# Seven chunks of a three-block fp32 network turned by DMA transposes in place of TensorE's, and two parameter loads moved behind a transpose

## What is computed

```python
qa, ka, va, qs, ks, vs = jnp.split(h @ even_w_in, idx, axis=-1)     # layer one's input chunks
...
xb = h @ odd_w_in[:, D:]                                            # layer two
xc = conv_b + sum(conv_w[j] * shift(xb, 3 - j) for j in range(4))   # causal, four taps
r = sigmoid(xc @ gate_w[0] + gate_b[0]); i = sigmoid(xc @ gate_w[1] + gate_b[1])
y = gelu(h @ odd_w_in[:, :D]) * lru_scan(r, i * xc)
```

## Time and profile before

| | |
|---|---|
| median of 3 runs | 3118.76 us (3118.72 to 3119.77) |
| the profiled execution, its own time | 3119.9 us |
| its span | 3118.1 us, 37400 instructions |
| TensorE | 3102.8 us, 14684 matmuls |
| VectorE | 1984.4 us |
| ScalarE | 1557.6 us |
| GpSimd | 265.8 us |
| DMA | 621.55 MB, 199 GB/s |
| TensorE's clock granted | full in every slice (2.4 GHz) |

### The profile page before, as it was taken

How to read it: one execution, slowest core, us unless ns; L and a number is a source line. 1 busy time by engine, 2 the same in 40 slices (tenths; PEclk the granted TensorE clock), 3 DMA queues, 4 the chain that set the end, 5 groups by cost and what they waited for, 6 DMA issues and landing times.

```text
span 3118.1 us, 37400 instructions
## 1 busy us (share of the span) xinstructions
PE 3102.8 (100%) x14684; PEld 2574.0 (83%) x14684; DVE 1984.4 (64%) x2278; ACT 1557.6 (50%) x2157; POOL 265.8 (9%) x330
## 2 busy tenths in 40 slices
PE   9999999999999999999999999999999999999999
PEld 8788888888888888878888888888888888888887
DVE  6677765656565768676574655568986555555455
ACT  6666543444444669554443434563455443444344
POOL 0000000000000020010830006720000000000000
PEclk9999999999999999999999999999999999999999
DMA  7455676766667555667676766777655766666664
GB/s 244 143 158 168 190 221 189 218 201 206 207 201 227 166 186 187 213 184 214 200 214 187 219 201 222 245 230 222 203 155 170 211 204 205 197 201 208 188 211 155
DMA packets 408623, 621.55 MB, mean 199 GB/s; under 512 B 112848, under 2 KB 124544, under 8 KB 408448
## 3 DMA queue, kind: packets, MB, share of 16 engines
q1 hardware_dynamic: 403056, 612.52, 64.3%
q10 hardware_dynamic: 5392, 6.64, 0.7%
HBM read 587.09 MB, written 11.01 MB: 192 GB/s over the span
## 4 chain that ended last, share of the span: by engine, by line
PE 95%; DVE 3%; ACT 1%; issue 1%; DMA 0%; SPq 0%; ACTq 0%; DVEq 0%
PE pair L2303 30%; PE pair L2305 30%; PE pair L2304 30%; DVE lo L1412 1%; PE turn_ps L2334 1%; PE pair L2733 0%; DMA turned_bytes<-tmp 0%; ACT hi L697 0%; PE misc_ps L2639 0%; DVE xt_hl L1761 0%; PE misc_ps L2653 0%; PE pair L2271 0%; PE pair L2622 0%; PE pair L2624 0%; PE pair L2623 0%
## 5 line engine op out<-in xcount | busy, mean ns | idle before, releaser
L1412 DVE TENSOR_TENSOR lo<-raw,hi 128x1024 fp32r<-128x1024 f32 x1084 | 1337.6, 1247 | 713.8 <-ACT hi L697 701.7
L697 ACT ACTIVATE hi<-raw 128x1024 fp32r<-128x1024 f32 x1084 | 1128.9, 1057 | 871.5 <-PE pair L2305 860.3
L2303 PE MATMUL pair<-hi,xt_hl 128*128 128x512 f32 (+1 forms) x2780 | 1089.8, 392 | 5.3 <-DVE lo L1412 3.5
L2305 PE MATMUL pair<-lo,xt_hl 128*128 128x512 f32 (+1 forms) x2780 | 1079.6, 388 | 0.0
L2304 PE MATMUL pair<-hi,xt_hl 128*128 128x512 f32 (+1 forms) x2780 | 1078.8, 388 | 0.0
L2303 PEld LDWEIGHTS pair<-hi,xt_hl 128*128 128x128 f32 x2780 | 522.1, 188 | 117.8 <-DVE lo L1412 5.1
L2305 PEld LDWEIGHTS pair<-lo,xt_hl 128*128 128x128 f32 x2780 | 521.9, 188 | 108.7
L2304 PEld LDWEIGHTS pair<-hi,xt_hl 128*128 128x128 f32 x2780 | 522.4, 188 | 103.6
L2303 PE MATMUL pair<-hi,ht_h 128*128 128x512 f32 x1504 | 586.7, 390 | 0.1
L2305 PE MATMUL pair<-lo,ht_h 128*128 128x512 f32 x1504 | 585.2, 389 | 0.0
L2304 PE MATMUL pair<-hi,ht_l 128*128 128x512 f32 x1504 | 585.2, 389 | 0.0
(11 more groups left out here) (343 smaller groups left out, 1717.6 us busy)
## 6 DMA issues: line engine op xcount, KB each, us to landing
raw<-in_mlp_w SPq DMA_DIRECT2D x512, 512.0 KB, 4.5
raw<-in_w_gate SPq DMA_DIRECT2D x88, 512.0 KB, 4.4
raw<-in_w_up SPq DMA_DIRECT2D x88, 512.0 KB, 4.2
raw<-in_w_down SPq DMA_DIRECT2D x88, 512.0 KB, 4.4
raw<-in_even_w_in SPq DMA_DIRECT2D x68, 512.0 KB, 4.2
raw<-in_odd_w_in SPq DMA_DIRECT2D x64, 512.0 KB, 4.2
raw<-in_w_in SPq DMA_DIRECT2D x64, 512.0 KB, 4.5
raw<-in_even_w_out SPq DMA_DIRECT2D x32, 512.0 KB, 4.2
```

What stands on the lines that cost most here:

```text
L697: nc.scalar.activation(hi[:, r], raw[:, slot], ACT.Copy).then_inc(sems["hi_ready"], 1)
L1412: nc.vector.tensor_tensor(lo[:, r], raw[:, slot], hi[:, r].bitcast(F32), ALU.subtract).then_inc(sems["lo_ready"], 1)
L2303: nc.tensor.matmul(to, xh[:, t0 + k, tok], h[:, k], start=s, stop=False)
L2305: mm = nc.tensor.matmul(to, xh[:, t0 + k, tok], l[:, k], start=False, stop=e)
```

## The change

Seven chunks go the second way: in layer one the chunks with c = 7, 0, 2 and 1, in layer two the convolution's chunks 1, 2 and 3. They carry n = -1, which tells them from the MLPs' chunks. Their transpose lands in `stg` itself (`turned_stg`), which is free once it is parted. From there `bytes_join` writes layer one's chunks straight to `qk0`, and the convolution's to `joined`, which lies in `tmp`. The convolution's first tap (`bytes_conv`, ScalarE) and the others then read `joined`, after j = 3, 4 and 5 in place of 2, 3 and 4, and `ht_h` and `ht_l` follow at j = 6.

ScalarE's evacuation waited for the last split in every chunk once there had been a join; now it does so only in a chunk with a parted chunk before it (`stg_till`). `bytes_part` also waits for ScalarE's evacuation. S5's parameters are loaded behind the transpose that goes out in the third chunk of the second MLP (`load_b_raw`).

```diff
@@ -335,6 +335,8 @@
         states = [h_re, h_im]
         glu_z = [at("glu_z0", 192, [4, SEQ]), at("glu_z1", 196, [4, SEQ])]
         turned_bytes = [at(f"turned_bytes{j}", 112 + 4 * j, [4 * M, 2 * P], U16) for j in range(4)]
+        turned_stg = stg[:].rearrange("p m n -> p (m n)").bitcast(U16).rearrange("p (a b) -> p a b", a=4 * M)
+        joined = tmp[:].rearrange("p m n -> p (m n)").rearrange("p (k s) -> p k s", k=4)
         yt_h, yt_l = at("yt_h", 144, [8, SEQ], F32R), at("yt_l", 152, [8, SEQ], F32R)
         assert base + int(205.5 * K) <= 229344
 
@@ -447,10 +449,10 @@
             setup = params = chunk = gates = s5_params = glu = final = mix_at = heads_at = prepare = nothing
 
             def turn_slot(self, prev, units, kind):
-                if prev is None or prev.kind in ("flip", "bytes"):
+                if prev is None or prev.kind == "flip" or prev.kind == "bytes" and prev.to[0] != "conv":
                     return -1
                 if prev.to[0] == "conv":
-                    return 2
+                    return 3 if prev.kind == "bytes" else 2
                 return 4 if prev.kind == "rope" or prev.kind == "gelu" == kind else min(3, units - 2)
 
             def lead_psum(self, k):
@@ -530,12 +532,13 @@
             def bytes_turn(self, part):
 
                 self.eng.wait_ge(sems["parted"], self.T.add("parted"))
-                nc.sync.dma_start_transpose(turned_bytes[part][:].rearrange("p a (b t) -> p (a b) t", t=P),
+                to = turned_bytes[part][:] if part >= 0 else turned_stg
+                nc.sync.dma_start_transpose(to.rearrange("p a (b t) -> p (a b) t", t=P),
                                             tmp[:].rearrange("p m n -> p (m n)").bitcast(U16)
                                             ).then_inc(sems["bytes_turned"], 16)
 
             def chunk(self, kind, w, units=8, width=CH, lead=None, slot=None, prep=None, order=None,
-                      n=0, apart=False, **_):
+                      n=0, apart=False, params=False, **_):
                 src, t0, col0 = w
                 if lead and lead.kind == "post":
                     self.T.add("x_ready", len(TILES))
@@ -550,19 +553,20 @@
                     self.unit(src[:, tiles, cols], width)
                     if j == 1 and self.apart[0] is not None:
                         self.bytes_turn(self.apart[0])
+                        if params:
+                            self.load_b_raw()
                     if prep is not None:
                         self.prepare(prep, j)
                     if slot is not None:
                         self.mix_at(slot + j)
                 self.apart = self.apart[1], n if apart else None
 
-            def s5_params(self, step):
-
-                if step == 0:
-                    self.eng.wait_ge(sems["x_ready"], self.T.at("x_ready"))
-                    for ri, name in enumerate(("b_re_2", "b_im_2")):
-                        self.eng.dma_start(b_raw[:, ri], i[name][0].rearrange("(t g) n q -> (g n) t q", g=2)
-                                           ).then_inc(sems["b_raw_loaded"], 16)
+            def load_b_raw(self):
+
+                self.eng.wait_ge(sems["x_ready"], self.T.at("x_ready"))
+                for ri, name in enumerate(("b_re_2", "b_im_2")):
+                    self.eng.dma_start(b_raw[:, ri], i[name][0].rearrange("(t g) n q -> (g n) t q", g=2)
+                                       ).then_inc(sems["b_raw_loaded"], 16)
 
             def prepare(self, g, j):
 
@@ -707,8 +711,9 @@
                 if by == "psum_free_act":
                     if m == 0:
                         self.eng.wait_ge(sems["turned"], T.at("turned"))
-                        if T.any("joined"):
-                            self.eng.wait_ge(sems["split_done"], T.at("split_done"))
+                        if self.stg_till:
+                            self.eng.wait_ge(sems["split_done"], self.stg_till)
+                            self.stg_till = 0
                         if kind == "gelu":
                             self.eng.wait_ge(sems["staged"], T.at("staged"))
                         self.eng.wait_ge(sems["half_used"], T.at("half_used"))
@@ -852,7 +857,13 @@
                                 self.load_gain(16 + k, i["final_g_2"][k * CH:(k + 1) * CH])
                         if prev and prev.kind == "bytes":
                             if j == 3:
-                                self.bytes_hi(prev)
+                                if prev.width >= 0:
+                                    self.bytes_hi(prev)
+                                elif prev.to[0] == "conv":
+                                    self.bytes_conv(prev)
+                                else:
+                                    T.add("split_done")
+                                self.stg_till = T.at("split_done")
                         elif j == at:
                             self.split(prev.to)
                         if j == 0 and prev and prev.kind == "flip":
@@ -888,6 +899,20 @@
                     return Pending(kind, ps, to, width)
                 if kind in ("add", "set", "sum", "first") and ss:
                     self.unsquared = n
+
+            stg_till = 0
+
+            def bytes_conv(self, prev):
+
+                T, t0 = self.T, prev.to[1]
+                self.eng.wait_ge(sems["joined"], T.add("joined"))
+                self.eng.wait_ge(sems["split_done"], T.at("split_done"))
+                for k in range(4):
+                    w, b = C_CONV_W + 48 + t0 + k, C_CONV_B + t0 + k
+                    a = nc.scalar.activation(conv_o[:, k], joined[:, k], ACT.Identity, scale=col[:, w:w + 1],
+                                             bias=col[:, b:b + 1])
+                a.then_inc(sems["conv_begun"], 1)
+                T.add("split_done")
 
             def bytes_hi(self, prev):
 
@@ -1479,7 +1504,7 @@
                 T = self.T
                 T.add("turned")
                 if to[0] == "conv":
-                    return self.conv_tap(to[1], 0)
+                    return self.conv_tap(to[1], 0, turn_ps)
                 if to[0] == "lru":
                     self.eng.wait_ge(sems["turned"], T.at("turned"))
                     self.eng.wait_ge(sems["lru_scanned"], to[1] // 4 + 1)
@@ -1503,8 +1528,9 @@
             def bytes_part(self):
 
                 T = self.T
-                self.eng.wait_ge(sems["psum_free_dve"], T.at("psum_free_dve"))
-                self.eng.wait_ge(sems["staged"], T.at("staged"))
+                for name in ("psum_free_dve", "psum_free_act", "staged"):
+                    if T.any(name):
+                        self.eng.wait_ge(sems[name], T.at(name))
                 halves = stg[:].rearrange("p m n -> p (m n)").bitcast(U16).rearrange("p (n two) -> p two n", two=2)
                 planes = tmp[:].rearrange("p m n -> p (m n)").bitcast(U16).rearrange("p (two n) -> p two n", two=2)
                 for half in range(2):
@@ -1516,13 +1542,19 @@
 
                 T = self.T
                 self.eng.wait_ge(sems["bytes_turned"], T.add("bytes_turned", 16))
-                src = turned_bytes[prev.width][:].rearrange("p a (b t) -> p (a b) t", t=P)
-                to = stg[:].rearrange("p m n -> p (m n)").bitcast(U16).rearrange("p (k m t two) -> p m k t two", k=4, m=M, two=2)
+                own = prev.width >= 0
+                src = (turned_bytes[prev.width][:] if own else turned_stg).rearrange("p a (b t) -> p (a b) t", t=P)
+                if own:
+                    to = stg[:].rearrange("p m n -> p (m n)").rearrange("p (k s) -> p k s", k=4)
+                else:
+                    to = joined if prev.to[0] == "conv" else prev.to[1]
+                to = to.bitcast(U16).rearrange("p k (m t two) -> p m k t two", m=M, two=2)
                 for half in range(2):
                     a = nc.vector.tensor_copy(to[:, :, :, :, half],
                                               src[:, 8 * half:8 * half + 8].rearrange("p (m k) t -> p m k t", m=M))
-                a.then_inc(sems["joined"], 1)
-                T.add("joined")
+                told = "joined" if own or prev.to[0] == "conv" else "split_done"
+                a.then_inc(sems[told], 1)
+                T.add(told)
 
             def bytes_lo(self, prev):
 
@@ -1556,7 +1588,7 @@
                                         prev.to[0].bitcast(F32), ALU.subtract).then_inc(sems["split_done"], 1)
                 T.add("split_done")
 
-            def conv_tap(self, t0, j):
+            def conv_tap(self, t0, j, src):
 
                 T = self.T
                 if j:
@@ -1566,7 +1598,7 @@
                 s = 3 - j
                 for k in range(4):
                     c = C_CONV_W + 16 * j + t0 + k
-                    a = nc.vector.scalar_tensor_tensor(conv_o[:, k, s:SEQ], turn_ps[:, k, 0:SEQ - s],
+                    a = nc.vector.scalar_tensor_tensor(conv_o[:, k, s:SEQ], src[:, k, 0:SEQ - s],
```

(17 more changed lines are left out.)

## The result

The changed kernel takes 3132.44 us (median; 3131.33 to 3134.73), the kernel before 3119.45 beside it: ratio 1.0039 (1.0029 to 1.0049), slower by 12 to 13 us where I forecast +5.3. It lies above the range of 3114 to 3130. The profiled execution took 3131.53 us for a span of 3129.6.

What follows compares the result with a forecast made beforehand. TensorE was taken to bound the kernel (95% of the chain). Gains of 3.6, 2.2 and 0.5 us against 11.6 lost in the convolution made +5.3 us: 3124.1 us from the median 3118.76, just within no change; range 3114 to 3130.

Steps and rivals of the forecast that it cites:

- Layer one, 3.6 us: Layer one's four chunks: taking the transposes off TensorE gains the full 0.89 us each, 3.6 us; bounds 0 and 3.6.
- the evacuation, 0.5: Gelu chunks: dropping ScalarE's wait for the last split gains 0.5 us; bounds 0 and 0.6.
- S5's parameters, 2.2 us: Second MLP: S5's loads placed behind the transpose can't delay it, so TensorE's stall goes, gaining 2.2 us.
- Convolution, three chunks, 11.6 us lost: Convolution: late transposes delay the gate units, costing 2.0, 2.0 and 6.4 us, plus 1.2 for the joins.
- Landing 4.9 us, the median of the earlier trace: Convolution transposes assumed to land 4.9 us after issue; bounds 4.5 and 7.9.
- rival 1: Convolution's three joins: transposes land late, 1.5 us each, 4.5 in all, giving 3128.6 us; chance 0.15.
- the load goes out at 1128.16: Convolution: this load takes 0.37 us, so the transpose is issued behind it at 1128.5 and lands at 1133.4.
- rival 2: Convolution: GpSimd holds VectorE's joins, costing 2.3 us in all in place of 1.2, giving 3125.2 us; chance 0.25.
- Third chunk, 6.4 us: Third convolution chunk: ScalarE's LRU decay falls between first and last taps, so the gate units begin 6.4 us later.
- Join allowance, 0.4 each: Convolution joins: 0.4 us added to each for GpSimd's nearby gate operations, 1.2 in all; bounds 0 and 1.4 a join.
- Taps priced alike from SBUF and PSUM: Convolution taps: VectorE's fused operations priced alike, 0.486 us from SBUF against 0.47 each from PSUM.
- The gain of 0.8 us a chunk: Convolution: by the skill's fixed costs, twelve VectorE taps from SBUF estimated 0.8 us cheaper a chunk; not used in the price.

Runs made afterwards that it cites:

- e2: The changed kernel with its three convolution chunks turned on TensorE again and S5's two loads back ahead of the next chunk's loads: 3115.39 us, ratio 0.9984.
- e1: The changed kernel with its three convolution chunks turned on TensorE again, layer one and S5's loads as changed: 3112.86 us, ratio 0.9976.
- e3: The changed kernel with each convolution transpose issued just ahead of the second load instead of just behind it: 3129.58 us, ratio 1.0031.
- e7: e1 with layer one's four transposes issued directly behind the third load instead of some 1.8 us behind the second: 3112.12 us, ratio 0.9975.
- e8: e4 with GpSimd's sum into lru_h waiting for the first gate instead of the second: 3122.23 us, ratio 1.0007.
- e4: The changed kernel with each convolution transpose issued behind the gate units' two loads, two loads sooner: 3129.37 us, ratio 1.0029.
- e5: e4 with only the first and second convolution chunks by DMA, the third back on TensorE: 3119.78 us, ratio 0.9999.
- e12: e9 with the first taps one weight unit later and GpSimd's sum for the last gates back behind both gates: 3113.45 us, ratio 0.9979.
- e6: The changed kernel with its third convolution chunk back on TensorE: 3122.92 us, ratio 1.0007.
- e9: e8 with only the first and second convolution chunks by DMA: 3117.61 us, ratio 0.9992.

## Why the prediction was wrong

- **Layer one, 3.6 us, and the evacuation, 0.5:** right as far as can be told. e2 measures 5.0 us for the two (2.2 to 7.8 by its interval), and in the changed kernel's trace layer one is 3.9 us shorter and the 0.6 us wait is gone. The transposes landed 1 us sooner than I took.
- **S5's parameters, 2.2 us:** right, 2.5 by e1 and e2. My reason was only partly tested. I blamed the two parameter loads; the transpose of the earlier trace rows also had a 512 KB load 0.4 us ahead of it, from start to start. Moving the loads ends the stall in either case. It also moved that 512 KB load to 1.2 us ahead, and there the transpose landed in 5.2.
- **Convolution, three chunks, 11.6 us lost: the step that failed.** It measured 19.6. The mechanism stood (no cover, join, taps, ht_l, the gates wait, the third chunk worst), but three of its terms were off. With the 2.7 us of turning that it takes off, the forecast had 14.3 us of TensorE's waits and nothing for the clock; the trace has 16.7 us and 4.9. The waits for ht_l, forecast at about 2, 2 and 6 us, were 2.3, none and 6.6. Of the 8.0 us missed, 2.4 are waits, 4.9 the clock, and 0.7 stand in no row:
  - *Landing 4.9 us, the median of the earlier trace rows.* It was 6.0 to 7.7. That is rival 1, which named the place and the slope. I spoke against it with packets and mean DMA load. What decides is the load issued 0.4 us ahead of the transpose (e3 and e7), and this was to be read in my own step "the load goes out at 1128.16". Of the 38 transposes before, 37 start 1.2 to 1.4 us behind the start of a load and land in 4.5 to 7.9. One starts 0.4 us behind it, that of the earlier trace rows (the second of the two loads starts at 1369.65), and its row alone would have given the right size:

```profile
1367.24 2.78 SPq L525 DMA_DIRECT2D raw<-in_mlp_w  x2
1370.06 5.31 SPq L533 DMA_TRANSPOSE turned_bytes<-tmp  x1
...
DMA to landing us min/median/max: 7.3/7.3/7.3
```

  - *Only ht_l was followed to TensorE.* Behind the late join and first tap stands a lo that TensorE wants before the gates: 7.8 of the 16.7 us. Landing in time doesn't end this wait: e3's transposes landed in 3.7 us, and TensorE waited 3.3 us for lo, since the joins were held. Only with the joins back at 1.37 us (e8) is it gone. So the late buffer has a second consumer, which neither rival 1 nor rival 2 had priced.
  - *The clock was taken to stay at 1.00.* It cost 4.9 us, and this is the largest part of the miss. Better landings alone would not have saved it: e3 lost 4.0.
- **Third chunk, 6.4 us:** 6.6 us of waiting for ht_l, 1.7 for a lo, and 1.8 of the clock behind them, less 0.9 of turning. The step's order of taps, decay, ratio and low parts is the one in the trace.
- **Join allowance, 0.4 each (rival 2):** 0 in the changed kernel, where the joins came after GpSimd's operations and took 1.39 us. In e3 and e4, where the transposes are on time, it is 2.1 to 2.2 us in the second chunk. I had priced 0.8, with lru_x ending at 1134.2 and the join wanted at 1133.4. The first of e4's two copies took 2.95 us beside it. The sentence of the Trainium skill, "SBUF — State Buffer", section "SBUF: two separate sides", that the first to start gets the shared port pair for its whole instruction, agrees: that copy started 0.9 us after lru_x and ended 0.6 us after it did.
- **Taps priced alike from SBUF and PSUM:** right for VectorE, four take 1.66 us from SBUF and took 1.64 from PSUM. The gain of 0.8 us a chunk, my estimate by the Trainium skill, "VectorE: DVE Perf Modes", section on the TRN2 errata, isn't there. For ScalarE its table has the right sign and size, 0.2 us by my estimate: four first taps take 2.08 us instead of 1.93. That estimate's 1.5 us in all doesn't follow from its terms either; three chunks of 0.8 less 0.2 are 1.8.

**What stays open.** Why e3, with 3.7 us to landing, and e4, with 7.8 in the second chunk, both meet the same held join is clear: the one lands at 1132.9 and the other at 1130.8, and the lo ahead of the join ends at 1132.9 and 1132.5. Why a transpose behind the two gate loads lands in 6.3 to 8.6 us (e4, e5, e8 to e12), while the MLPs' in the trace before, at the same 1.2 us behind one load, have a median of 4.9, no run separates: it can be two loads so close together or the gate weights' pieces. Not tried was a transpose that is both early and without a load ahead of it, nor a lru_x that starts behind the join. The table leaves up to 1.1 us unexplained in e3 and e4. When the clock falls I can't say from these runs: it fell in or behind waits of 2.1 to 6.6 us. But the changed kernel's first wait, of 3.3 us, left it at 1.00 where e6's, of 3.5 us, did not, and e8's first, of 2.2 us, left it at 1.00 where e9's of the same length did not.

## What to carry to other kernels

Price a DMA by the rows of its kind that stand in the same place in the queue, not by their median: a transpose that starts 0.4 us behind a 512 KB load's start takes nearly twice as long to land (5.8 to 8.3 us) as one that starts 2.0 to 2.2 us behind it (3.6 to 4.3). Follow a late buffer to every consumer of the engine that it delays, and where the bounding engine will wait for microseconds, allow for the clock's fall in or behind the wait; not every wait here brought one. A unit of work moved off an engine at its bound is worth its time only where the chain that replaces it fits into the run-ahead. Here 0.9 us a chunk was bought with a chain of 11.7 us, and even with the transpose, the sum and the taps moved, and the third chunk left to TensorE (e12), it comes out level.

## What the runs showed of the hardware that I had not expected

- How long a DMA transpose from SBUF to SBUF of this size takes to land goes with the load ahead of it on the queue, counted from start to start: 3.6 to 4.3 us with 2.0 us or more between (layer one, e3), 4.5 to 7.9 with 1.2 to 1.4 us (the 37 of the trace before, median 4.9), 5.8 to 8.3 with 0.4 us (the changed kernel, e6, e7). Its issue holds the queue for 1.6 to 2.2 us in the first case, 2.4 to 4.3 in the second and 3.7 to 5.4 in the third. The ranges overlap, so the distance isn't all of it.
- VectorE's 16-bit copies of a join, 0.74 us each alone, take up to 2.95 us beside one GpSimd multiplication of 128x1024 (e4); the taps of the kernel before, which read PSUM, are not held: 1.64 us at 1134.88, beside lru_x.
- TensorE's clock stayed at the lower level for 3 to 7 us behind single waits of 2.1 to 3.5 us, in kernels whose mean granted clock is 0.997 to 0.999.
